# Two of three sigmoid gates as seven block products each, with the operand sums kept in memory that is dead at that time

## The reference, cut to what matters

```
proj = einsum('bsd,dc->bsc', x, w_in)                    # x (1, 512, 1024)
cb, cc, ch, hq, hf, hi, hg, mq, ga, gb, gc = split(proj)   # ga, gb, gc: 1024 columns each
y_a, y_b, y_c = conv(...), hgrn2(...), attention(...)      # (1, 512, 512) each
merged = (sigmoid(ga + b_ga) * (y_a @ w_branch[0])         # (512x512) @ (512x1024)
        + sigmoid(gb + b_gb) * (y_b @ w_branch[1])
        + sigmoid(gc + b_gc) * (y_c @ w_branch[2]))
x = layer_norm(ALPHA * x + merged @ w_o, ln1_g, ln1_b)
h = square(relu(x @ w_up))
out = layer_norm(ALPHA * x + h @ w_down, ln2_g, ln2_b)
```

## Time and profile before

| | |
|---|---|
| median of 3 runs | 827.91 us (827.8 to 827.98) |
| the profiled execution's own time | 827.88 us |
| its span in the trace | 826.0 us |
| mean granted TensorE clock | 0.997 of 2.4 GHz |
| TensorE busy | 815.8 us, 99% |
| VectorE busy | 500.7 us, 61% |
| ScalarE busy | 353.2 us, 43% |
| GpSimd busy | 31.1 us, 4% |
| HBM read | 84.96 MB, 105 GB/s over the span |

### The profile page before, as it was taken

How to read it: one execution, slowest core, us unless ns; L and a number is a source line. 1 busy time by engine, 2 the same in 40 slices (tenths; PEclk the granted TensorE clock), 3 DMA queues, 4 the chain that set the end, 5 groups by cost and what they waited for, 6 DMA issues and landing times.

```text
span 826.0 us, 10117 instructions
## 1 busy us (share of the span) xinstructions
PE 815.8 (99%) x4059; PEld 690.2 (84%) x4059; DVE 500.7 (61%) x556; ACT 353.2 (43%) x405; POOL 31.1 (4%) x38
## 2 busy tenths in 40 slices
PE   9999999999999999999999999999999999999996
PEld 8889888898888888888888889888888888888884
DVE  4647555476454433424428685896579656955698
ACT  5558324593334224222225035643554355435532
POOL 1100100000001000000000010000000000000005
PEclk9999999999999999999999999999999999999998
DMA  9641312313122322233723407018201820280002
GB/s 311 202 152 52 102 55 98 102 51 102 51 102 95 110 78 79 98 100 102 305 102 106 148 4 252 1 52 290 66 1 55 294 60 1 69 287 1 1 1 102
DMA packets 67223, 87.52 MB, mean 106 GB/s; under 512 B 1613, under 2 KB 49782, under 8 KB 67190
## 3 DMA queue, kind: packets, MB, share of 16 engines
q1 hardware_dynamic: 67190, 87.06, 31.4%
HBM read 84.96 MB, written 2.10 MB: 105 GB/s over the span
## 4 chain that ended last, share of the span: by engine, by line
PE 96%; DVE 2%; DMA 1%; SPq 0%; issue 0%; ACT 0%; DVEq 0%
PE bank L1375 31%; PE bank L1377 31%; PE bank L1376 31%; DMA raw<-in_w_mem_k_dram 1%; PE bank L1591 0%; PE bank L1541 0%; PE bank L1659 0%; PE bank L1402 0%; PE bank L1512 0%; DVE two L1245 0%; DVE smx L1251 0%; PE bank L1594 0%; PE bank L1579 0%; PE bank L1543 0%; PE bank L1548 0%
## 5 line engine op out<-in xcount | busy, mean ns | idle before, releaser
L1375 PE MATMUL bank<-x_hi,w_hi 128*128 128x512 f32 (+1 forms) x704 | 268.4, 381 | 0.0
L1376 PE MATMUL bank<-x_lo,w_hi 128*128 128x512 f32 (+1 forms) x704 | 267.2, 380 | 0.0
L1377 PE MATMUL bank<-x_hi,w_lo 128*128 128x512 f32 (+1 forms) x704 | 267.2, 379 | 0.0
L820 DVE TENSOR_TENSOR w_lo<-raw,w_hi 128x2048 fp32r<-128x2048 f32 x40 | 91.5, 2293 | 108.1 <-ACT w_hi L516 107.9
L1377 PEld LDWEIGHTS bank<-x_hi,w_lo 128*128 128x128 f32 x704 | 132.4, 188 | 25.0
L1375 PEld LDWEIGHTS bank<-x_hi,w_hi 128*128 128x128 f32 x704 | 132.4, 188 | 24.7
L1376 PEld LDWEIGHTS bank<-x_lo,w_hi 128*128 128x128 f32 x704 | 132.5, 188 | 24.5
L1375 PE MATMUL bank<-w_hi,y_hi 128*128 128x512 f32 x304 | 118.6, 390 | 0.0
L1377 PE MATMUL bank<-w_hi,y_lo 128*128 128x512 f32 x304 | 118.3, 389 | 0.0
L1376 PE MATMUL bank<-w_lo,y_hi 128*128 128x512 f32 x304 | 118.3, 389 | 0.0
L516 ACT ACTIVATE w_hi<-raw 128x2048 fp32r<-128x2048 f32 x40 | 76.4, 1915 | 37.8 <-PE bank L1377 36.8
(11 more groups left out here) (194 smaller groups left out, 840.2 us busy)
## 6 DMA issues: line engine op xcount, KB each, us to landing
raw<-in_w_in_dram SPq DMA_DIRECT2D x28, 1024.0 KB, 5.0
raw<-in_w_up_dram SPq DMA_DIRECT2D x16, 1024.0 KB, 7.1
small<-in_w_down_dram SPq DMA_DIRECT2D x12, 1024.0 KB, 7.1
raw<-in_w_branch_dram SPq DMA_DIRECT2D x6, 1024.0 KB, 5.1
raw<-in_w_o_dram SPq DMA_DIRECT2D x4, 1024.0 KB, 5.0
raw<-in_w_down_dram SPq DMA_DIRECT2D x4, 1024.0 KB, 4.7
small<-in_w_mem_v_dram SPq DMA_DIRECT2D x4, 512.0 KB, 10.7
two<-in_x_dram SPq DMA_DIRECT2D x2, 1024.0 KB, 12.1
```

What stands on the lines that cost most here:

```text
L820: dve.tensor_tensor(w_lo[:, slot, :], raw[:, r, :], w_hi[:, slot, :].bitcast(F32), ALU.subtract)\
L1375: pe.matmul(dst, a[0], b[0], start=first, stop=False, skip_group_check=goes_on)
L1376: pe.matmul(dst, a[0], b[1], start=False, stop=False, skip_group_check=goes_on)
L1377: return pe.matmul(dst, a[1], b[0], start=False, stop=last, skip_group_check=goes_on)
```

## The change

The first gate is computed as before. The second and third are each computed with a seven-product scheme over 2 x 2 blocks: tokens in two halves of 256, input features in two halves of 512, output features in two halves of 512. Each product is 512 input features x 512 output features x 256 tokens, in place of eight such products.

- TensorE: per product two pairs of 128 features, with 4 blocks of input and three matmuls of 256 columns each (`seven_product`); results accumulate in banks 4 and 5, 6 and 7, or 0 and 1. The two branch slabs f0 and f1 are as before (`branch_tiles`). The order is m1, m5, m6, m3, m2, m7, f0, m4, f1, slots 0 to 2 in turn. The loops are written out.
- Weights: the four blocks A, B, C and R of a gate's matrix are loaded whole (A into `gate_a`, B into `gate_b`, C in two parts into `gate_c`, R through `raw`). VectorE makes the sums A + C (m5), A + C + B (m6), B + C (m7) and A + C + B + R (m4) in place (`seven_add`). `gate_a` and `gate_b` are slot 3 of `w_hi` and `w_lo`; `gate_c` is the first 256 tokens of the first four blocks of `x_hi` and `x_lo`, which after the first gate only exist as part of sums.
- Tokens: four sums and differences of quarters of x (128 x 1024 each) are made once at the start of the first gate (`x_forms_made`), rounded and split (`x_forms_low`), and kept in the first 4096 numbers of `two` and in those of `ln_par`.
- Results: ScalarE copies m1, m5 and m6 out of PSUM (`copied`), the following products keep adding in the same banks, and VectorE adds or subtracts m3, m2 and m7 from the copies (`added`). m4's bank goes straight into a sigmoid. The merge of the second half of the features is in two pieces of 256 tokens (`second_merge`).
- x is loaded again in two parts, after m3 and after m7 of the third gate, and the norm parameters in two parts, after m5 and m6.

```diff
 S_PROJ, N_PROJ = 4, len(PROJ)
 S_GATE, N_GATE = S_PROJ + 2 * N_PROJ, 6
-S_OUT = S_GATE + 3 * N_GATE
+N_SEVEN = 9
+S_OUT = S_GATE + N_GATE + 2 * N_SEVEN
 S_MLP, N_MLP = S_OUT + 4, 11
...
+SEVEN = ("m1", "m5", "m6", "m3", "m2", "m7", "f0", "m4", "f1")
+GATE_SUMS = ("m5", "m6", "m7", "m4")
+COPIED = ("m1", "m5", "m6")
+ADDED = ("m3", "m2", "m7")
...
+        def gate_block(i, k, n):
+            at = i * D + COL["gate"] + (2 - n) * WID
+            return win[:, (k - 1) * PAIRS:k * PAIRS, at:at + WID]
...
-            with sp.Fori(0, 3) as i:
-                for h in range(2):
-                    for j in range(2):
-                        load(i * N_GATE + (S_GATE + 3 * h + j), (3 * h + j) % 2,
-                             win[:, :, ds(i * D + (COL["gate"] + h * WID + j * 256), 256)], KD)
-                    load(i * N_GATE + (S_GATE + 3 * h + 2), (3 * h + 2) % 2,
-                         wbr[:, ds(i * HEADS, HEADS), h * WID:(h + 1) * WID], HEADS)
...
+            def a_load(i):
+                if i == 1:
+                    sp.wait_ge(x_form_split, 4)
+                else:
+                    sp.wait_ge(slab_lo, seven_slab(i - 1, "m4") + 1)
+                sp.dma_start(as_block(gate_a), gate_block(i, 1, 1)).then_inc(gate_a_landed, 16)
+            def b_load(i):
+                if i == 1:
+                    sp.wait_ge(x_form_split, 4)
+                else:
+                    sp.wait_ge(slab_lo, seven_slab(i - 1, "m3") + 1)
+                    sp.wait_ge(gate_sums, seven_sum(i - 1, "m7"))
+                sp.dma_start(as_block(gate_b), gate_block(i, 2, 2)).then_inc(gate_b_landed, 16)
+            def c_load(i):
+                if i == 1:
+                    sp.wait_ge(tile_done, gate_round(0) * MAIN + 12)
+                    sp.wait_ge(x_formed, 4)
+                else:
+                    sp.wait_ge(slab_lo, seven_slab(i - 1, "m7") + 1)
+                for e in range(2):
+                    sp.dma_start(gate_c[e], gate_block(i, 1, 2)[:, :, e * 256:(e + 1) * 256]).then_inc(gate_c_landed, 16)
+            for r in range(3):
+                plain_load(0, r)
+            plain_load(1, 0)
+            plain_load(1, 1)
+            a_load(1)
+            b_load(1)
+            plain_load(1, 2)
+            ring(seven_ring(1, "m2"), S_GATE + 4, gate_block(1, 2, 1), PAIRS)
+            branch_load(1, 0, seven_ring(1, "f0"), S_GATE + 5)
+            c_load(1)
+            b_load(2)
+            branch_load(1, 1, seven_ring(1, "f1"), seven_slab(1, "m2"))
+            c_load(2)
+            ring(seven_ring(2, "m2"), seven_slab(1, "f0"), gate_block(2, 2, 1), PAIRS)
+            a_load(2)
+            branch_load(2, 0, seven_ring(2, "f0"), seven_slab(1, "f1"))
+            branch_load(2, 1, seven_ring(2, "f1"), seven_slab(2, "m2"))
...
+            sp.wait_ge(gate_done, seven_done(2, "m5", 1))
+            par_load(0, ln1_g)
+            par_load(1, ln1_b)
+            x_reload(0, "m3")
+            out_load(0, seven_slab(2, "f0"))
+            x_reload(2, "m7")
+            out_load(1, seven_slab(2, "f1"))
+            out_load(2, S_OUT)
+            out_load(3, S_OUT + 1)
+            sp.wait_ge(gate_done, seven_done(2, "m6", 1))
+            par_load(2, ln2_g)
+            par_load(3, ln2_b)
...
+                seven_hi(i, "m6")
+                act.wait_ge(merge_done, 1 + i * KD)
+                act.wait_ge(vhalf_ready, 2)
+                copied(i, "m1", lambda c: late[:, c:c + 2, :], 1.0)
+                seven_hi(i, "m3")
+                copied(i, "m5", lambda c: tiles4[:, c:c + 2, 0:256], 1.0)
+                seven_hi(i, "m2")
+                copied(i, "m6", lambda c: tiles4[:, c:c + 2, 256:512], -1.0)
+                seven_hi(i, "m7")
+                seven_hi(i, "f0")
+                seven_hi(i, "m4")
+                for c in range(4):
+                    act.wait_ge(gate_added, seven_added(i, "m2", c // 2))
+                    act.activation(late[:, c, :], late[:, c, :], ACT.Sigmoid, bias=bias(1, c)).then_inc(gate_sig, 1)
+                seven_hi(i, "f1")
+                for c in range(4):
+                    act.wait_ge(gate_added, seven_added(i, "m7", c // 2))
+                    act.activation(tiles4[:, c, :], tiles4[:, c, :], ACT.Sigmoid, bias=bias(0, c)).then_inc(gate_sig, 1)
...
+            def seven_add(i, name):
+                if name != "m7":
+                    dve.wait_ge(slab_lo, seven_slab(i, dict(m5="m1", m6="m5", m4="m6")[name]) + 1)
+                if name == "m5":
+                    dve.wait_ge(gate_a_landed, 16 * i)
+                    dve.wait_ge(gate_c_landed, 32 * i)
+                    for e in range(2):
+                        to = as_block(gate_a)[:, :, e * 256:(e + 1) * 256]
+                        st = dve.tensor_tensor(to, to, gate_c[e], ALU.add)
+                elif name == "m7":
+                    dve.wait_ge(gate_b_landed, 16 * i)
+                    dve.wait_ge(gate_sums, seven_sum(i, "m5"))
+                    for e in range(2):
+                        st = dve.tensor_tensor(gate_c[e], gate_c[e], as_block(gate_b)[:, :, e * 256:(e + 1) * 256], ALU.add)
+                elif name == "m6":
+                    dve.wait_ge(gate_b_landed, 16 * i)
+                    st = dve.tensor_tensor(gate_a, gate_a, gate_b, ALU.add)
+                else:
+                    n = seven_ring(i, "m2")
+                    dve.wait_ge(slab_landed[n % 2], ring_landed(n))
+                    st = dve.tensor_tensor(gate_a, gate_a, raw[:, n % 2, :], ALU.add)
+                st.then_inc(gate_sums, 1)
+            def x_forms_made():
+                dve.wait_ge(tile_done, gate_round(0) * MAIN)
+                halves = [[x[:, k:k + PAIRS, :].rearrange("p k (a t) -> p k a t", a=2).bitcast(F32) for x in (x_hi, x_lo)]
+                          for k in (0, PAIRS)]
+                def whole(to, k):
+                    return dve.tensor_tensor(to.rearrange("p (a k t) -> p k a t", a=2, k=PAIRS), *halves[k], ALU.add)
+                whole(gate_a, 0).then_inc(form_link, 1)
+                whole(gate_b, 1).then_inc(form_link, 1)
+                a21, a11, a22, a12 = form_of["m7"], form_of["m6"], form_of["m5"], form_of["m3"]
+                dve.wait_ge(form_link, 2)
+                dve.tensor_tensor(a22, a21, a22, ALU.subtract).then_inc(x_formed, 1)
+                dve.tensor_tensor(a21, a11, a21, ALU.subtract).then_inc(x_formed, 1)
+                dve.wait_ge(x_formed, 1)
+                dve.tensor_tensor(a11, a22, a11, ALU.subtract).then_inc(x_formed, 1)
+                dve.wait_ge(x_formed, 3)
+                dve.tensor_tensor(a12, a11, a12, ALU.add).then_inc(x_formed, 1)
...
+                x_forms_made()
+                for h in range(2):
+                    if h == 0:
+                        lo(S_GATE + 2, 2)
+                        lo(S_GATE + 3, 0)
+                        x_forms_low()
+                        lo(S_GATE + 4, 1)
+                    else:
+                        lo(S_GATE + 5, 2)
+                        seven_lo(1, "m1")
+                    dve.wait_ge(merge_done, 4 * h + 1)
...
+                        if h and t == 1:
+                            seven_add(1, "m5")
+                        elif h and t == 2:
+                            seven_lo(1, "m5")
+                seven_add(1, "m6")
...
+                seven_lo(i, "m6")
+                seven_add(i, "m7")
+                seven_lo(i, "m3")
+                seven_add(i, "m4")
+                seven_lo(i, "m2")
+                seven_lo(i, "m7")
+                added("m3", tiles4[:, :, 256:512], ALU.add)
+                seven_lo(i, "f0")
+                added("m2", late, ALU.add)
+                seven_lo(i, "m4")
+                added("m7", tiles4[:, :, 0:256], ALU.subtract)
+                seven_lo(i, "f1")
+                for c in range(4):
+                    first_merge(c)
+                if last:
+                    ring_lo(S_OUT, R_OUT, 0)
+                    merged_parts(0)
+                    ring_lo(S_OUT + 1, R_OUT + 1, 1)
+                    second_merge(0)
+                    second_merge(1)
+                    ring_lo(S_OUT + 2, R_OUT + 2, 3)
+                    second_merge(2)
+                    second_merge(3)
+                    return
+                seven_lo(i + 1, "m1")
+                seven_add(i + 1, "m5")
+                second_merge(0)
+                seven_lo(i + 1, "m5")
+                second_merge(1)
+                seven_add(i + 1, "m6")
+                second_merge(2)
+                second_merge(3)
 
...
+            def seven_product(i, name):
+                slot = SEVEN.index(name) % 3
+                opens = name in DOWN_OPENS
+                slab(seven_slab(i, name))
+                if name in x_forms:
+                    pe.wait_ge(x_form_split, 4)
+                for p in range(2):
+                    if name == "m1" and i == 1:
+                        aux_copied(pe, HALF, "out%d" % p, 1)
```

(71 more changed lines are left out.)

266 lines of the change are left out of this document (211 added, 55 removed).

## The result

The changed kernel takes 821.63 us (median of 4 runs, 821.23 to 821.95) against 827.87 us (4 runs, 827.8 to 827.98): ratio 0.9924, 95% interval 0.9911 to 0.9936. The forecast was 821.5 us. The profiled execution took 821.65 us with a span of 819.9 us, 6.1 us less than before (6.16 before rounding).

The account below looks back on a forecast made before the run. The prediction took TensorE's matmul stream as the bound: 3.20 us less in each of two gates, 6.40 in all, with supply and reload at nothing, takes 827.88 us to 821.48, predicted as 821.5; range 820.8 to 824.6.

Parts of the forecast that it names:

- The bound: In the three gates, TensorE's matmul issue sets the length: 65.28 us each, TensorE busy throughout.
- 192 x 226.7 ns for 336 x 120.0 ns: Second and third gates: own matmuls take 40.32 us in place of 43.52, saving 3.20 us a gate.
- the same 13.3 ns: TensorE's stream: each matmul start distance is its columns at 2.4 GHz plus 13.3 ns, at 512 and 256 columns.
- The rival by columns plus 2.5 ns: New gates' matmuls issue at columns plus 2.5 ns, saving 9.5 us: 818.4 us; chance 0.04.
- Supply: Operands for the new gates' slabs are ready in time; this is where the 6.4 us could be lost.
- The three places with the least room: First gate's third slab 3.5 us, bank 0 after its first merge 2.8, second gate's m6 0.8.
- late at the entry: Second gate's entry: C lands late, TensorE stands 3.2 us, 824.7 us; chance 0.22 together with small stalls.
- VectorE as the bound: New gates: VectorE's 46.5 us plus in-order waits lengthen gates towards 65.3 us, time towards 827.9; chance 0.07.
- The weight loads, the slower side: New gates: every matmul waits for its full 0.19 us weight load, 45.7 us more, 867 us; chance 0.04.
- My point of decision, 129.5 ns: New gates: the distance between matmul starts at which the gain is gone.
- The reload costed at nothing: x and norm parameters, loaded again during third gate and output projection, first used at 445 us, cost nothing.
- The sum: Whole kernel: two gates at 3.20 us less each, 6.40 us in all, giving span 819.6 us.

Follow-up runs that it names:

- experiment 4: Changed kernel with the first gate's 192 matmuls of 512 columns issued as 384 of 256 columns: 824.27 us.
- experiment 8: Changed kernel with each first-gate tile issued in parts of 384 and 128, or 320 and 192 columns: 830.68 us, a single execution.
- experiment 1: Changed kernel with block C of the second gate's matrix loaded 5.4 us later, after the first gate's tile 13 instead of 11: 825.22 us.
- experiment 6: Changed kernel with the first sum of x's forms made three times more, 6.7 us of additional VectorE work ahead of the first gate's third slab: 826.82 us.
- experiment 5: Changed kernel with half of the two new gates' own matmuls left out, other work kept, output not the layer's: 793.97 us.
- experiment 3: Changed kernel with product m1 of both new gates issued as 96 matmuls of 128 columns in place of 48 of 256: 831.63 us.
- experiment 7: Changed kernel with x and the norm parameters loaded again only after the output projection's four slabs: 821.59 us.
- experiment 2: Changed kernel with block C loaded after all tiles of the first gate, 10.9 us later: 830.6 us.

## Why the prediction was right

- *The bound.* TensorE's stream sets the gate: 65.28 us from one gate's first start to the next became 62.12, and 288 more matmuls changed nothing else in the chain.
- *192 x 226.7 ns for 336 x 120.0 ns.* Forecast 3.20 us a gate, measured 3.16. Experiments 4 and 8 show the same 13.3 ns in another gate and at two other widths. The rival by columns plus 2.5 ns, which would have given 9.5 us, did not come: the starts are 120 ns apart.
- *Supply.* The three places with the least room came out at their times: the first gate's third slab ready at 265.2 (265.3 forecast), the first merge at 275.74 (276.2), m6's remainder at 323.14 (323.0). Experiments 1 and 6 measured two of the rooms by using them up: 0.8 us as forecast, and 3.7 where 3.5 was forecast (the remainder ends 7.0 us later than in the changed kernel, measured from the start of the gate, where 6.7 was expected, and the slab starts 3.3 later). Experiment 1's 4.0 us late sum for 3.2 us of waiting is the "late at the entry" rival with its price; it did not happen, since C landed at 307.2, 1.4 us before VectorE was free for it.
- *VectorE as the bound.* It did not come. With half of the products gone, the gates still last 50.72 and 45.82 us (experiment 5), against 62.1 in the real kernel: TensorE's own work would have to shrink by some 11 and 16 us before VectorE's chain decides the gate's length. A late operand at the entry decides much sooner (experiment 1).
- *The weight loads, the slower side.* At 256 columns they do not bind, but if they are what sets the floor, they are closer than I thought: it is 111.6 ns, and the prediction, with 13.3 ns as a price of any width, would have missed most of the 10.0 us at 128 columns: it gave 1.3 (experiment 3). My point of decision, 129.5 ns, stands; the price I gave this rival, 190 ns, was that of loads that do not overlap, and no run showed such a one.
- *The reload costed at nothing.* Right, and so it stays when it is issued at 431 us, behind the output projection's slabs (experiment 7).
- *What was off.* The sum said 6.40 us, the spans differ by 6.16: 0.11 to 0.12 us from the start of the kernel, 0.08 from the two gates (62.12 for 62.08), 0.05 from the end. And I priced a wait of TensorE at its own length; experiment 6 shows that a wait of 3.2 us in front of a full stream can cost 5.1.

No run tells what a single new gate, or a seven-product first gate, would give; neither was tried. No run that does all the work was faster than the changed kernel by more than its runs differ.

## What to carry to other kernels

A scheme that trades eight products for seven saves by columns, but pays per matmul: count both at the distances of starts that the same shapes show in the trace, here 12.5% of the columns but 7.4% of the time (40.3 for 43.5 us). Then play out each operand's chain, with its in-order queues, against the time at which TensorE wants it; the smallest room is the real risk, and one load issued 11 us later turned this gain into a loss. A busy share of 77% on the helping engine says nothing on that.

## What was not expected of the hardware

- A floor of 111.6 ns between matmuls of 128 and 192 columns, each with its own weights, with weight loads overlapping at the same pace; of the widths tried, 256 columns are the narrowest that keep to their columns plus 13.3 ns. The Trainium skill (TensorE: Matmul & The Clock Gate, LDWEIGHTS) gives 107 ns for a load of 128 columns. The distance of the starts in experiment 3 is 5 ns above that; the records of the loads themselves are 0.19 us long, so the trace neither shows nor excludes that this is the load's own time.
- After a wait of 3.17 us TensorE's clock was at 1.2 GHz for some matmuls, which cost 1.7 us more (experiment 6). In the traced execution of experiment 1, waits of 0.95 and 1.84 us left it at 2.4; four of its ten runs took on average 1.4 us more, at a lower mean clock, so this may not hold for every execution. In a wait of 6.35 us the clock fell too, and what that cost was hidden behind the next late operand (experiment 2).
- Something in the first 17 us moves the whole kernel by up to 0.8 us from one execution to the next (204.14 to 204.96 at the same matmul). The landing of the first loads is the likely cause: TensorE waits there for the first loads (`two<-in_mem_dram`) 0.38 us in the kernel before, 0.93 in the changed one and 1.67 in experiment 2's, the latest of the ten. No experiment shows it, and not every difference at 17 us is in these waits.
